# Head norms of q and k in three rounds of four, and their rotation four heads at a time, in a two-layer hybrid decoder step

## The reference, cut to what matters

```python
def rmsnorm(x, g):
    y = xf * lax.rsqrt(jnp.mean(xf * xf, axis=-1, keepdims=True) + EPS)
    return (y * g.astype(jnp.float32)).astype(x.dtype)

def rope(x, pos):
    x1, x2 = xf[..., :half], xf[..., half:]
    return jnp.concatenate([x1 * cos - x2 * sin, x2 * cos + x1 * sin], axis=-1)
...
    proj = xn @ w_in
    u, q, k, v, qi, ki, wi, gl = jnp.split(proj, np.cumsum(IN_SIZES).tolist(), axis=-1)
    q = rope(rmsnorm(q.reshape(nb, s, N_HEADS, HEAD_DIM), q_norm), pos)      # 8 heads of 128
    k = rope(rmsnorm(k.reshape(nb, s, N_KV_HEADS, HEAD_DIM), k_norm), pos)   # 4 heads of 128
...
    y_att = attend(q, k, v, qi, ki, wi, pos)
    y_ssm, h_re, h_im = s5_scan(u, h0_re, h0_im, ...)
    gates = jax.nn.sigmoid(gl)
```

## Time and profile before

| | before |
|---|---|
| median of 3 runs | 3014.46 us (3014.34 to 3015.56) |
| span of the profiled execution | 3013.6 us |
| TensorE busy | 2976.0 us, 99% of the span |
| VectorE busy | 1966.5 us, 65% |
| ScalarE busy | 1249.4 us, 41% |
| GpSimd busy | 253.7 us, 8% |
| granted TensorE clock | 1.000 of full speed |

### The profile page before, as it was taken

How to read it: one execution, slowest core, us unless ns; L and a number is a source line. 1 busy time by engine, 2 the same in 40 slices (tenths; PEclk the granted TensorE clock), 3 DMA queues, 4 the chain that set the end, 5 groups by cost and what they waited for, 6 DMA issues and landing times. The chain is left out here.

```text
span 3013.6 us, 58619 instructions
## 1 busy us (share of the span) xinstructions
PE 2976.0 (99%) x23480; PEld 2851.8 (95%) x23480; DVE 1966.5 (65%) x3145; ACT 1249.4 (41%) x1763; POOL 253.7 (8%) x239
## 2 busy tenths in 40 slices
PE   8999999999999999999999999999999999999999
PEld 7988888999999999999999888889999999999999
DVE  7669788577665545555576697985776565455653
ACT  4443334543544333434344433344444543333332
POOL 4420001300000000000034200013000000000000
PEclk9999999999999999999999999999999999999999
DMA  7557444755655655556555573446555556455564
GB/s 263 170 156 200 138 143 162 235 169 174 201 181 182 202 167 180 182 183 206 185 203 172 159 200 122 155 165 221 181 182 191 184 182 202 163 183 183 181 207 137
DMA packets 150623, 546.45 MB, mean 181 GB/s; under 512 B 19872, under 2 KB 25632, under 8 KB 149952
## 3 DMA queue, kind: packets, MB, share of 16 engines
q1 hardware_dynamic: 137728, 507.40, 50.6%
q0 software_dynamic: 12096, 35.67, 4.7%
q10 hardware_dynamic: 640, 1.16, 0.1%
HBM read 536.95 MB, written 7.21 MB: 181 GB/s over the span
## 5 line engine op out<-in xcount | busy, mean ns | idle before, releaser
L1840 DVE TENSOR_TENSOR w_ffn_low<-ring_ffn,w_ffn_high 128x1024 fp32r<-128x1024 f32 (+1 forms) x480 | 638.6, 1331 | 457.1 <-ACT w_ffn_high L1344 457.1
L1344 ACT ACTIVATE w_ffn_high<-ring_ffn 128x1024 fp32r<-128x1024 f32 (+1 forms) x480 | 548.0, 1142 | 641.8 <-PE main L1053 638.9
L1051 PE MATMUL main<-x_ffn_high,w_ffn_high 128*128 128x264 f32 x2816 | 791.7, 281 | 0.0
L1052 PE MATMUL main<-x_ffn_low,w_ffn_high 128*128 128x264 f32 x2816 | 791.3, 281 | 0.0
L1053 PE MATMUL main<-x_ffn_high,w_ffn_low 128*128 128x264 f32 x2816 | 791.3, 281 | 0.0
L1051 PEld LDWEIGHTS main<-x_ffn_high,w_ffn_high 128*128 128x128 f32 x2816 | 526.6, 187 | 0.1
L1052 PEld LDWEIGHTS main<-x_ffn_low,w_ffn_high 128*128 128x128 f32 x2816 | 526.6, 187 | 0.1
L1053 PEld LDWEIGHTS main<-x_ffn_high,w_ffn_low 128*128 128x128 f32 x2816 | 526.6, 187 | 0.0
L1051 PE MATMUL main<-hidden_high,w_ffn_high 128*128 128x264 f32 x1408 | 395.6, 281 | 0.0
L1052 PE MATMUL main<-hidden_low,w_ffn_high 128*128 128x264 f32 x1408 | 395.6, 281 | 0.0
L1053 PE MATMUL main<-hidden_high,w_ffn_low 128*128 128x264 f32 x1408 | 395.6, 281 | 0.0
(11 more groups left out here) (375 smaller groups left out, 4819.1 us busy)
## 6 DMA issues: line engine op xcount, KB each, us to landing
ring_ffn<-in_w_up SPq DMA_DIRECT2D x352, 512.0 KB, 3.3
ring<-in_w_in SPq DMA_DIRECT2D x260, 512.0 KB, 3.9
ring_ffn<-in_w_down SPq DMA_DIRECT2D x128, 704.0 KB, 4.1
ring<-in_w_br SPq DMA_DIRECT2D x64, 512.0 KB, 3.2
ring<-in_w_out SPq DMA_DIRECT2D x64, 512.0 KB, 3.3
w_low<-in_w_in POOLq DMA_DIRECT2D x20, 512.0 KB, 6.9
ring<-in_w_glu SPq DMA_DIRECT2D x16, 512.0 KB, 3.9
out_x<-x SPq DMA_DIRECT2D x7, 528.0 KB, 5.9
```

The source lines that it names most:

```text
L1051: mm(out, wfh[:, slot, w], high[:, kk, :], start=kk == 0, stop=False)
L1052: mm(out, wfh[:, slot, w], low[:, kk, :], start=False, stop=False)
L1344: af(wfh[:, s, 0:cols], ring_ffn[:, s, 0:cols], ACT.Copy).then_inc(high_ready, 1)
L1840: tt(wfl[:, s, 0:cols], ring_ffn[:, s, 0:cols], wfh[:, s, 0:cols].bitcast(F32), ALU.subtract).then_inc(low_ready, 1)
```

## The change

The sums of squares are made in three rounds. ScalarE squares four heads in one operation of 1,056 columns, and TensorE makes four products, each with 32 output rows, that land in rows 0, 32, 64 and 96 (and the 31 behind each) of one bank. The spreading is made in three rounds of four products as well, each with 32 input rows, into four banks. VectorE waits once for each round. Block 49 is laid between these rounds in parts of 6, 2 + 4 and 4 pieces.

The rotation is made four heads at a time: ScalarE writes the two crossed halves (`swap_halves(b)`: two operations of 64 partitions and 1,056 columns), and VectorE multiplies by the sine, multiplies by the cosine and adds (`rotate(b)`: three operations of 1,056 columns). `rotate(0)` stands ahead of `skip(0)`. `swap_halves(2)` stands between the copies of `bu(1)`, and so do the high copies of the units 103 to 105, at other places than before.

`s5_in(1)` takes four pieces with each round instead of six, block 52 goes where block 53 was, and block 53 goes into the attention loop, which has 24 units instead of 22. In the scan `attend` begins two scan steps later, before step 3. The wait `act.wait_ge(units, 106)` ahead of `coefficients(1)` is not changed.

```diff
--- before.py
+++ after.py
...
-                    return (22 * u + 9) // 18
+                    return (24 * u + 9) // 18
...
-                    def sum_heads(first, last):
-                        for t in range(first, last + 1):
-                            if t == 0:
-                                pe.wait_ge(one_hot_made, 1)
-                            pe.wait_ge(qsq_ready, t + 1)
-                            mm(side[0][:, 0:T], one_hot[:, NHK - 1 - t:NHK - 1 - t + P], sq[:, t % 2, :],
-                               start=t == 0, stop=t == NHK - 1).then_inc(qsum_ready, 1)
+                    def sum_heads(r):
+
+                        if r == 0:
+                            pe.wait_ge(one_hot_made, 1)
+                        pe.wait_ge(qsq_ready, r + 1)
+                        for q in range(4):
+                            m = mm(side[0][32 * q:32 * q + 32, 0:T], one_hot[:, NHK - 1 - r:NHK - 1 - r + 32], acc[:, q, :],
+                                   start=r == 0, stop=r == 2)
+                        m.then_inc(qsum_ready, 1)
 
                     spread_rows(0)
-                    sum_heads(0, 5)
+                    sum_heads(0)
                     spread_rows(1)
-                    sum_heads(6, 8)
+                    sum_heads(1)
                     fill(1)
-                    sum_heads(9, NHK - 1)
+                    sum_heads(2)
                     fill(2)
                     pe.wait_ge(spread_used, 6)
-                    for t in range(NHK):
-                        if t == 0:
-                            pe.wait_ge(qinv_ready, 1)
-                        if t >= 4:
-                            pe.wait_ge(qnormed, t - 3)
-                        mm(side[t % 4][:, 0:T], ident[:, t:t + 1].to_broadcast([P, P]), rs[:, 0, :],
-                           start=True, stop=True).then_inc(qinv_spread, 1)
-                        if t in (5, NHK - 1):
-                            fill(1)
+                    pe.wait_ge(qinv_ready, 1)
+
+                    def spread_heads(r):
+
+                        if r:
+                            pe.wait_ge(qnormed, 4 * r)
+                        for q in range(4):
+                            rows, at = slice(32 * q, 32 * q + 32), 32 * q + r
+                            m = mm(side[q][:, 0:T], ident[rows, at:at + 1].to_broadcast([32, P]), rs[rows, 0, :], start=True, stop=True)
+                        m.then_inc(qinv_spread, 1)
+
+                    spread_heads(0)
+                    w_in_piece(49, 0, 6)
+                    spread_heads(1)
+                    w_in_piece(49, 6, 2)
+                    w_in_piece(49, 8, 4)
+                    spread_heads(2)
+                    w_in_piece(49, 12, 4)
                     pe.wait_ge(qnormed, NHK)
                     pe.wait_ge(cneg, 1)
                     s5_out(0)
                     pe.wait_ge(y_added, 4)
-                    s5_in(1, 50, 6)
+                    s5_in(1, 50, 4)
...
-                    w_in_blocks(53, 1)
+                    w_in_blocks(52, 1)
...
+                    def swap_halves(b):
+
+                        act.wait_ge(qnormed, 4 * b + 4)
+                        if b:
+                            act.wait_ge(qroped, 4 * b)
+                        heads = proj[:, K + 4 * b:K + 4 * b + 4, :]
+                        af(acc[0:HD // 2], heads[HD // 2:HD], ACT.Copy, scale=-1.0)
+                        af(acc[HD // 2:HD], heads[0:HD // 2], ACT.Copy).then_inc(qswapped, 1)
...
-                            if half == 1 and v in (9, 13, 17):
-                                highs_to(103 + v // 4 - 2)
+                            if half == 1 and v in (9, 17, 25):
+                                highs_to(103 + v // 8 - 1)
+                            if half == 1 and v == 5:
+                                swap_halves(2)
...
-                    for t in range(NHK):
-                        if t >= 2:
-                            act.wait_ge(qsum_ready, t - 1)
-                        if t < 1:
-                            act.wait_ge(proj_copied, 34)
-                        af(sq[:, t % 2, :], proj[:, K + t, :], ACT.Square).then_inc(qsq_ready, 1)
-                        if t == 1:
+                    act.wait_ge(proj_copied, 34)
+                    for r in range(3):
+                        if r:
+                            act.wait_ge(qsum_ready, r)
+                        af(acc, proj[:, K + 4 * r:K + 4 * r + 4, :], ACT.Square).then_inc(qsq_ready, 1)
+                        if r == 0:
                             highs_to(94)
-                        if t == 5:
+                        if r == 1:
                             evac_gates(46, 1)
                             highs_to(95)
-                        if t == 10:
-                            act.wait_ge(gix_ready, 1)
-                            highs_to(96)
-                        if t == 11:
-                            highs_to(97)
-                            evac_gates(47, 1)
+                    act.wait_ge(gix_ready, 1)
+                    highs_to(97)
+                    evac_gates(47, 1)
                     load_root()
-                    act.wait_ge(qsum_ready, NHK)
+                    act.wait_ge(qsum_ready, 3)
                     af(rs[:, 0, :], side[0][:, 0:T], ACT.Sqrt, bias=small[:, 7:8], scale=1.0 / HD).then_inc(qstd_ready, 1)
                     highs_to(98)
                     highs_to(99)
                     evac_gates(48, 1)
                     highs_to(100)
+                    swap_halves(0)
                     evac_gates(49, 1)
                     highs_to(101)
+                    swap_halves(1)
                     act.wait_ge(y_ready, 4)
...
-                    evac_gates(50, 4)
+                    evac_gates(50, 3)
...
-                        dve.wait_ge(qinv_spread, t + 1)
+                        dve.wait_ge(qinv_spread, t // 4 + 1)
...
+                    def rotate(b):
+
+                        tiles = proj[:, K + 4 * b:K + 4 * b + 4, :]
+                        dve.wait_ge(qswapped, b + 1)
+                        turned = tmp[:].rearrange("p (k t) -> p k t", t=T)
+                        st.mark(tt(turned, turned, sinq.unsqueeze(1).to_broadcast([P, 4, T]), ALU.mult))
+                        st.link(tt(tiles, tiles, cosq.unsqueeze(1).to_broadcast([P, 4, T]), ALU.mult))
+                        tt(tiles, tiles, turned, ALU.add).then_inc(qroped, 4)
+
                     lows_to(100)
+                    dve.wait_ge(qnormed, NHK)
+                    rotate(0)
                     skip(0)
                     lows_to(101)
-                    dve.wait_ge(qnormed, NHK)
-                    for t in range(12):
-                        tile, buf = proj[:, K + t, :], th[:, t % 2, :]
-                        if t >= 2:
-                            dve.wait_ge(qroped, t - 1)
-                        st.mark(stt(buf[0:HD // 2], tile[HD // 2:HD], -1.0, sinq[HD // 2:HD], ALU.mult, ALU.mult))
-                        st.link(tt(buf[HD // 2:HD], tile[0:HD // 2], sinq[0:HD // 2], ALU.mult))
-                        st.link(tt(tile, tile, cosq, ALU.mult))
-                        tt(tile, tile, buf, ALU.add).then_inc(qroped, 1)
-                        if t % 2:
-                            lows_to(min(102 + t // 2, 105))
+                    rotate(1)
+                    lows_to(102)
+                    rotate(2)
+                    lows_to(105)
...
-                        u = n // 2
-                        if n % 2 or u > 2 * NH:
+                        u = n // 2 - 1
+                        if n % 2 or u < 0 or u > 2 * NH:
```

6 lines of the change are left out of this document (3 added, 3 removed).

## The result

The changed kernel takes 3029.8 us (median of 4 runs, 3028.9 to 3030.8) against 3014.9 us (3014.3 to 3015.6) for the kernel before: 14.9 us more, a ratio of 1.0049, 95% interval 1.0036 to 1.0061. Its profiled execution has a span of 3028.0 us, 14.4 more than before. (A run is 1.8 us longer than its own span here, 3029.82 against 3028.0, and not about one microsecond; since both kernels have it, it drops out of the difference.)

A forecast was written before the change was run, and what follows sets the result against it. TensorE, busy for 2976.0 of 3013.6 us, was the bound; 7.2 us a layer saved there came back as waits and a longer loop, losing 6.4 a layer, 12.8 on 3014.5: 3027 us, range 3016 to 3036.

The forecast's parts named there:

- the walk: Step-by-step timing of the first layer, handover by handover between engines: the layer loses 6.4 us, two layers 12.8.
- What comes off TensorE: Sums and spreads in rounds of four: 4.4 and 2.8 us saved, together 7.2 us a layer.
- steps 1 and 2: Sums, then spreads: waits of 0.4, 1.3 and 0.3 us, then 1.5 and 0.4, mostly for VectorE's low copies.
- Step 3: Behind s5_out(0): skip stands behind low copy 100 and rotate(0), so TensorE waits 3.1 us instead of 0.6, 2.5 more.
- Step 4: s5_in(1) rounds: 3.2 us wait at swap_halves(2), 1.6 for high copies; rounds end at 400.5, 3.2 ahead of before.
- Step 5: Ahead of the scan: coefficients wait for unit 105 (407.4), and the scan starts at 409.6, 2.3 us later than 407.31.
- Step 6: Attention loop: late masked logits and reciprocals bring waits of 4.2, 1.8 and 1.4 us; s5_out(1) starts at 515.4.
- The scan did not start early: Second rival: scan starts once its inputs are copied, at 402; loss 3.2 us a layer, 3021 us; chance 0.07.
- The wide operation is not cheap: First rival: wide rotation operations at 0.65 us and half-price swaps give 3017.5 us, no change; chance 0.07.
- The rounds run side by side: Third rival claimed the opposite: a round costs 1.76 us, loss 11.8 us a layer, 3038 us; chance 0.03.
- the fourth rival: TensorE's clock falls behind the new waits, 1 to 2 us each, two or three of six: 3031 us; chance 0.15.

The follow-up runs named there:

- x4: x3 with VectorE's rotations, the skip and ScalarE's program (but for the squares) as before the change: 3004.8 us, 0.9964 of the kernel before.
- x8: The kernel before with only the new layout of blocks, the high copies and the coefficients' wait (105 units) as in x4: 3012.4 us, ratio 0.9990.
- x2: The changed kernel with ScalarE's wait ahead of coefficients(1) at 105 units instead of 106: 3024.2 us, 1.0030 of the kernel before.
- x1: The changed kernel with attend's first masked logits put back to where the kernel before had them, two scan steps earlier: 3019.6 us, ratio 1.0014.
- x5: x3 with swap_halves(2) behind copy 11 instead of 5, and high copies behind copies 11, 19, 27 instead of 9, 17, 25: 3012.0 us, ratio 0.9987.
- x12: x5 with six extra unused products between s5_out(0) and the skip's wait, filling the wait of 2.6: 3009.7 us, ratio 0.9980.
- x6: x5 with the skip between the second and third operation of rotate(0), and the second swap behind copy 3 of bu(1): 3005.4 us, ratio 0.9967.
- x9: x4 with the first four heads rotated wide behind the skip, and the high copies at the ends of rounds: 2998.9 us, ratio 0.9948.
- x11: x4 with the high copies of bu(1) behind copies 11, 19 and 27 instead of 9, 17 and 25: 3004.6 us, ratio 0.9968.
- x3: The changed kernel with masks as before and coefficients one unit earlier (edits of x1 and x2): 3013.8 us, 0.9996 of the kernel before.

## Why the prediction was right, and what it missed

The forecast was 3027 (its own range 3022 to 3031), slower with 0.80; the measured time is 3029.8. The places of the walk stand in the trace within 0.8 us; two of its waits don't (1.99 for 3.2, and none for 1.8), and some of its errors cancel. Of the 2.8 us that it missed, 1.4 are the two layers (14.25 lost for 12.8), 0.4 is the kernel before (3014.9 beside the changed one, 3014.5 in the forecast), and the rest was not traced.

- **What comes off TensorE.** `s5_out(0)` was put at 370.9 and is at 370.80, the first spread at 360.9 and is at 360.68. A round of sums takes 0.58 (343.38 to the next product at 343.96), one of spreads 0.66 (360.68 to 361.34), in the 0.5 to 0.9 foretold. The row at 361.34, a whole-array product that starts 0.07 us ahead of the end of the round, shows no full drain, as the earlier trace rows had. A part of one may be there: passes of one kind overlap by 0.17 (0.39 long and 0.22 apart, from the sixteen in 3.72 of the earlier trace rows), and a round costs 0.1 to 0.2 more than the 0.48 that four products take inside L807. The ends of products are modelled in the trace, so this is a weak reading. The rule of the Trainium skill ("TensorEngine Tiling (Array Packing)", section "Key Properties") that a change of the tiling mode drains the array would have put each round a good part of a pass (0.39) higher; the trace bears it out in part at most. Of the 7.2 us a layer 3.8 reach the end (x4 against x8), mostly since the low copies of VectorE are then late, as steps 1 and 2 have it: waits of 0.94 and 1.23 us at L665.
- **Step 3** (2.5 more ahead of the first round of `s5_in(1)`): a wait of 2.60 where 0.59 stood, 2.0 more. The total of 3.1 was 0.5 too large, and no one price made it so: VectorE is there 0.2 earlier, and from start to start the low copy takes 1.14 for 1.25, `rotate(0)` 3.70 for 3.85 (its operations 1.16, 1.36 and 1.18), and the four `skip` operations 1.60 for 1.9.
- **Step 4**: the wait ahead of the third round is 1.99, not 3.2, mostly because TensorE came there 1.1 later (383.45 for 382.4) through the clock. That the round itself starts as foretold (385.44 for 385.6) is in part luck: `rotate(1)` ends at 382.0 where the walk had 383.0, but the second round's copies, late through the clock, keep ScalarE from `swap_halves(2)` for another 0.5. The three waits for high copies are 0.6 each, 1.8 in all for 1.6. The end of the rounds, 400.5 foretold, is 401.22. A round with its four pieces takes 2.31; the walk's own 0.8 + 1.46 is 2.26 and would have given 400.7, and it wrote down less.
- **Step 5**: coefficients, then the scan, at 409.6; it is 410.14. VectorE idle ahead of it for 10.5 us. x2 shows the cause: one unit less to wait for, 2.7 us of it back.
- **Step 6**: 4.2 ahead of the first `turn_probs`, 4.04 measured; `s5_out(1)` at 515.4, 515.95 measured. x1 shows the cause.
- **Rivals.** The scan did not start early. The wide operation is not cheap (1.16 to 1.36 for 1,056 columns, where the bound was 0.65). The rounds run side by side. The clock did fall, in each layer behind the waits of 2.60 and 4.04, four times where the rival had two or three, and yet it explains little of what the sum missed (7.0 and 7.3 us a layer instead of 6.4). In the first layer four pieces ran at half rate, 1.5 us, but the third round waits for ScalarE in any case, and only some 0.4 get through. The second layer shows it. There the clock fell later, in the first and second round, the swap was not held up (1.62 us of wait are left), and the third round starts 7.81 us behind the first instead of 8.20:

```profile
1884.70 0.73 PE L790 MATMUL side<-proj,bbt 32*128 32x264 f32 x8 [2.60 <-DVE proj L1699]
...
1892.51 0.73 PE L790 MATMUL side<-proj,bbt 32*128 32x264 f32 x8 [1.62 <-ACT arena L1220]
```

Behind the wait of 4.04 a unit took 5.41 us (3.72 at full rate), but VectorE's next probabilities were no earlier, so it cost little: the next wait, 1.8 in the walk, vanished. From the first `turn_probs` to `s5_out(1)` the first layer takes 91.6 us, just as in the walk. Its 0.55 too much are there at 424.35 already (423.8 foretold), and come down from the rounds' late end through the coefficients. In the second layer `s5_out(0)` to `s5_out(1)` takes 0.4 less than in the first; what it loses beyond the first lies ahead of `s5_out(0)`.

So the forecast came true by its mechanism. Of the fourth rival the falls of the clock came true, and not the price. What the prediction did not say is how little of the loss belongs to the headline of the change: without the late masks and the late coefficients, the wide rotations (+9.0) take back what rounds and blocks gain (-7.6 and -3.1).

The granted clock of 0.58 behind the wait of 2.60 us in x5 became 1.00 when the wait was filled (x12), for a gain of 2.3 us by the medians. The Trainium skill's advice against idle gaps between bursts of products ("TensorE: Matmul & The Clock Gate", section "Why this matters for your kernels") held there.

## What to carry to other kernels

When TensorE is 99% busy, price a change by the time at which each engine hands over, not by busy time: halving VectorE's rotations cost 9 us, because they ran where nobody waited, and their new order and ScalarE's swaps lay where TensorE did (laid otherwise, in x6, they cost nothing). When blocks of filler work move, look again at every constant that counts them (106 here) and at every step placed to match the old order: these two small edits cost 16 us. A buffer that two engines pass back and forth makes a chain of all its users; here the wide form paid only for the one group whose chain had slack (x9 against x11, 5.7 us less).

## What the hardware showed that was not expected

- A wait of 2.60 us ahead of the first round of `s5_in(1)` was followed by 3 to 7 us at half rate (0.42 for 0.28 us a product; 4.1 and 3.4 us a round for 2.3, x5), in both layers of each kernel that has it (the changed one, x1, x2, x3, x5). Filling it with useless products made x5 2.3 us faster by the medians.
- A wait of 1.75 was followed by half rate in the second layer of x5 and x12, and not in their first, nor in either layer of x6, nor was the 1.74 ahead of the loop in x11. The waits of 1.99 and 1.62 ahead of the changed kernel's third round were not followed by it either. The length of the wait alone doesn't tell; what else does was not tested.
- What a stretch at half rate costs hangs on the next wait: 1.5 us of it came to about 0.4 in the changed kernel, where ScalarE held the third round back anyway.
